# Norm squares summed in two rounded passes, low weight parts written over the loaded chunk, and another order of mixer steps, in a two-layer transformer kernel on one core

## What is computed

```python
def rms_norm(x, g):
    y = x * rsqrt(mean(x * x, axis=-1, keepdims=True) + 1e-6)
    return y * g

def mixer_block(h, ...):
    proj = rms_norm(h, norm1_g) @ w_in
    fq, fk, fv, ff, cq, ckv, krope, sq, sk, sv, gates = split(proj)
    fq, fk = rms_norm(fq per head of 64), rms_norm(fk per head of 64)
    log_decay = cumsum(log_sigmoid(ff + fox_forget_b))
    out_a = causal_attention(fq, fk, fv, log_decay)             # 8 heads (FOX)
    q = rope(rms_norm(rms_norm(cq) @ mla_w_q_up per head of 96))
    k, v_mla = from rms_norm(ckv) @ mla_w_kv_up and krope, k normed per head of 96, rope
    out_b = causal_attention(q, k, v_mla)                       # 8 heads (MLA)
    out_c = sliding_window_attention(rms_norm(sq), rms_norm(sk), sv, sinks, slopes)  # 8 heads (SWA)
    g = sigmoid(gates)
    return h + sum over branches(g * (out @ w_branch)) @ w_o

def conv_ffn(h, ...):
    u = rms_norm(h, norm2_g) @ w_up                             # 1024 to 5632
    c = conv_b + causal convolution of width 3 over tokens(u)
    gate, val = split(c)
    return h + (silu(gate) * val) @ w_down                      # 2816 to 1024
```

## Time and profile before

| what | before |
|---|---|
| median of three runs | 2064.24 us |
| the profiled execution, its own time | 2067.04 us |
| its span in the profile | 2065.2 us |
| PE busy | 1979.7 us (96%), 15080 matmuls |
| DVE / ACT / POOL busy | 1144.9 / 767.6 / 1023.8 us |
| mean granted PE clock | 0.988 of full speed |
| chain that ended last | PE 78%, DVE 11%, ACT 6%, issue 3% |

### The profile page before, as it was taken

One profiled execution on the slowest core, in us unless ns is written; L12 is line 12 of the kernel. 1 busy time (PEld: TensorE's weight loads), 2 busy tenths in 40 slices (PEclk: granted clock), 3 DMA queues, 4 the chain that ended last, 5 costly groups with the idle time before them and its releaser, 6 DMA issues.

```text
span 2065.2 us, 37779 instructions
## 1 busy us (share of the span) xinstructions
PE 1979.7 (96%) x15080; PEld 1879.0 (91%) x15080; DVE 1144.9 (55%) x2137; ACT 767.6 (37%) x1483; POOL 1023.8 (50%) x1306
## 2 busy tenths in 40 slices
PE   7899999899999999999998999999999999999999
PEld 7788997888999999999998889878889999999999
DVE  5665466676455665652356645656674656656411
ACT  4455566545222222220034555654452232222100
POOL 6755544443444444455476554543434445454543
PEclk9999999999999999999999999999999999999999
DMA  4112111111233323333332112111112323333332
GB/s 152 54 51 63 52 54 51 52 51 43 62 104 93 93 83 95 90 89 97 92 114 63 44 61 62 52 45 49 52 41 63 121 77 101 93 92 93 103 93 92
DMA packets 44803, 156.35 MB, mean 76 GB/s; under 512 B 5010, under 2 KB 5266, under 8 KB 44628
## 3 DMA queue, kind: packets, MB, share of 16 engines
q1 hardware_dynamic: 44484, 153.71, 24.6%
q10 hardware_dynamic: 144, 0.22, 0.0%
HBM read 149.58 MB, written 4.26 MB: 74 GB/s over the span
## 4 chain that ended last, share of the span: by engine, by line
PE 78%; DVE 11%; ACT 6%; issue 3%; DMA 0%; POOL 0%; ACTq 0%; DVEq 0%; SPq 0%
PE ps L1294 22%; PE ps L1297 21%; PE ps L1299 21%; PE ps L1528 5%; PE ps L1304 3%; DVE osum L1906 2%; DVE rstd L1619 1%; PE ps L1474 1%; PE ps L1435 1%; DVE ps L1876 1%; ACT xq L970 1%; DVE square L1614 1%; ACT square L987 1%; DVE q L1801 1%; ACT rstd L988 1%
## 5 line engine op out<-in xcount | busy, mean ns | idle before, releaser
L789 POOL TENSOR_TENSOR wl<-raw,wh 128x256 fp32r<-128x256 f32 x1080 | 800.6, 772 | 738.1 <-DVE wh L1598 729.9
L1294 PE MATMUL ps<-xh,wh 128*128 128x264 f32 (+1 forms) x2880 | 813.6, 304 | 5.8 <-POOL wl L789 2.7
L1297 PE MATMUL ps<-xl,wh 128*128 128x264 f32 (+1 forms) x2880 | 763.6, 285 | 0.0
L1299 PE MATMUL ps<-xh,wl 128*128 128x264 f32 (+1 forms) x2880 | 584.4, 284 | 0.0
L1294 PEld LDWEIGHTS ps<-xh,wh 128*128 128x128 f32 x2880 | 546.2, 190 | 32.7 <-issue 16.6
L1297 PEld LDWEIGHTS ps<-xl,wh 128*128 128x128 f32 x2880 | 546.5, 190 | 16.2 <-issue 7.2
L1299 PEld LDWEIGHTS ps<-xh,wl 128*128 128x128 f32 x2880 | 450.8, 190 | 0.0
L1598 DVE CAST wh<-raw 128x1024 fp32r<-128x1024 f32 x270 | 202.5, 750 | 166.1 <-PE ps L1294 152.2
L1898 DVE TENSOR_TENSOR ps<-ps,cst 128x128 f32<-128x128 f32 (+6 forms) x240 | 70.6, 296 | 209.7 <-PE ps L1480 139.6
L1297 PE MATMUL ps<-al,wh 128*128 128x264 f32 (+1 forms) x704 | 185.0, 283 | 0.0
L1294 PE MATMUL ps<-ah,wh 128*128 128x264 f32 (+1 forms) x704 | 183.6, 283 | 0.0
(11 more groups left out here) (183 smaller groups left out, 3208.1 us busy)
## 6 DMA issues: line engine op xcount, KB each, us to landing
raw<-weights SPq DMA_DIRECT2D x270, 512.0 KB, 3.6
h<-tokens SPq DMA_DIRECT2D x4, 528.0 KB, 6.5
h<-tokens SPq DMA_DIRECT2D x8, 264.0 KB, 5.3
residual<-h SPq DMA_DIRECT2D x8, 264.0 KB, 4.9
h<-residual SPq DMA_DIRECT2D x8, 264.0 KB, 5.9
out<-h SPq DMA_DIRECT2D x8, 256.0 KB, 4.7
cst<-constants SPq DMA_DIRECT2D x1, 1008.0 KB
extra<-positions SPq DMA_DIRECT2D x17, 4.1 KB
```

Source lines behind the costliest of these rows:

```text
L789: ins = nc.gpsimd.tensor_tensor(wl[c % SPLIT][:, part], raw[:, c % RAW, part], wh[c % SPLIT][:, part].bitcast(F32), ALU.subtract)
L1294: a = nc.tensor.matmul(out, a_hi, x_hi[:, sl], start=first, stop=False)
L1297: nc.tensor.matmul(out, a_hi, x_lo[:, sl], start=False, stop=False)
L1299: ins = nc.tensor.matmul(out, a_lo, x_hi[:, sl], start=False, stop=last)
```

## The change

**Squares in two parts.** ACT squares a normed tile twice from PSUM: first with a rounded output (`sqh`, fp32r), then in float32 (`sq`), and only then copies the tile to `rawt` (`mq` tiles have no copy). A new DVE step, "square low", subtracts one from the other in place and writes the rounded low part `sql` over `sq`. With `LAG` of -1 it stands on DVE directly behind the end of the tile, ahead of whatever else has that block position. The sum on PE waits for it (and for the copy, since it writes over the tile's PSUM) and is now two rounded passes, `sqh` and `sql`, against a rounded copy of the constants (`sums`), which ACT makes once at the start, over the float32 constants. The second pair of matmuls of an `mk` tile, the eight partial sums of the first residual norm and the sums of the residual norms stay float32.

**Low parts over the loaded chunk.** `raw` has four buffers instead of two, and POOL writes `wl` over `raw` in place; the three separate `wl` buffers are gone. A chunk of `raw` therefore stays in use until PE has multiplied by it: the load of chunk n now waits until PE has begun chunk n-3, which is one chunk later in SP's order than before (three chunks ahead of PE instead of four).

**Order.** `gF0` comes ahead of `fk0`, `fk1` ahead of `fq1`, `fq2` ahead of `fk2`, `gF2` ahead of `fq3`, `fv3` ahead of `gF3`, `gF6` ahead of `sq2`; `mv2` comes earlier and `mv3` later. Job 2 begins at block 127 instead of 121, jobs 1 and 11 one block later, jobs 7 and 8 two blocks earlier. The decay and rotation steps and a few lags move by some blocks.

```diff
@@ -32,7 +32,7 @@
-RAW, SPLIT = 2, 3
+RAW, SPLIT = 4, 3
...
-BEGIN = [65, 93, 121, 156, 192, 222, 250, 280, 318, 354, 391, 435]
+BEGIN = [65, 94, 127, 156, 192, 222, 250, 278, 316, 354, 391, 436]
...
-FIRST_LEAD, FIRST_STEP = 19, 1.0
-START = [16, 17, 16, 24, 30, 31, 2]
+FIRST_LEAD, FIRST_STEP = 16, 0.8
+START = [18, 18, 13, 21, 30, 32, 7]
...
             t.n = normed
             normed += 1
+            put(e + 1, 1, "square low", t)
...
+    raw_at = at[0]
     raw = sb("raw", [P, RAW, CW])
+    wl = sb("wl", [P, RAW, CW], F32R, offset=raw_at)
     wh = [sb(f"wh{i}", [P, CW], F32R) for i in range(SPLIT)]
-    wl = [sb(f"wl{i}", [P, CW], F32R) for i in range(SPLIT)]
...
+    sql = sb("sql", [P, 2, T], F32R, offset=sq_at)
+    sqh = sb("sqh", [P, 2, T], F32R)
...
+    sums = sb("sums", [P, 2 * P], F32R, offset=cst_at + CC_ONE * 4)
...
-                    sp.wait_ge(s_lo, n - RAW + 1)
+                    sp.wait_ge(s_start, n - RAW + 2)
...
-                    load(n // BLK + AHEAD + RAW)
+                    load(n // BLK + RAW - 1)
...
-                    ins = nc.gpsimd.tensor_tensor(wl[c % SPLIT][:, part], raw[:, c % RAW, part],
+                    ins = nc.gpsimd.tensor_tensor(wl[:, c % RAW, part], raw[:, c % RAW, part],
...
+            act.wait_ge(s_first, 16)
+            copy(sums[:, :], cst[:, CC_ONE:CC_ONE + 2 * P]).then_inc(sums_ready.sem, sums_ready.tick(()))
...
+                                nc.scalar.activation(sqh[0:MQ, t.n % 2, :], full(t.slot)[0:MQ, :], ACT.Square)
                                 nc.scalar.activation(sq[0:MQ, t.n % 2, :], full(t.slot)[0:MQ, :],
                                                      ACT.Square).then_inc(squared.sem, squared.tick((l, t.i)))
                             else:
+                                nc.scalar.activation(sqh[:, t.n % 2, :], full(t.slot), ACT.Square)
+                                nc.scalar.activation(sq[:, t.n % 2, :], full(t.slot),
+                                                     ACT.Square).then_inc(squared.sem, squared.tick((l, t.i)))
                                 for before in raw_before[t.i]:
                                     act.wait_ge(raw_taken.sem, raw_taken.at(l, before))
                                 copy(rawt[:, t.raw, :], full(t.slot)).then_inc(copied.sem, copied.tick((l, t.i)))
-                                nc.scalar.activation(sq[:, t.n % 2, :], full(t.slot),
-                                                     ACT.Square).then_inc(squared.sem, squared.tick((l, t.i)))
...
+            def stat_both(slot, i, lhs, rows, first=True, last=True):
+
+                stat(slot, sqh[0:rows, i, :], lhs[0:rows, :], first, False)
+                return stat(slot, sql[0:rows, i, :], lhs[0:rows, :], False, last)
...
-                        pe.wait_ge(squared.sem, squared.at(l, t.i))
-                        if t.kind == "mq":
+                        pe.wait_ge(square_low.sem, square_low.at(l, t.i))
+                        if t.kind != "mq":
+                            pe.wait_ge(copied.sem, copied.at(l, t.i))
+                        else:
                             pe.wait_ge(query_turned.sem, query_turned.at(l, t.i))
                         if t.kind == "cq":
-                            stat(t.slot, sq[:, (t.n - 1) % 2, :], ones, True, False)
-                            ins = stat(t.slot, sq[:, t.n % 2, :], ones, False, True)
+                            stat_both(t.slot, (t.n - 1) % 2, ones_r, P, True, False)
+                            ins = stat_both(t.slot, t.n % 2, ones_r, P, False, True)
                         elif t.kind == "mk":
                             if t.m == 0:
                                 pe.wait_ge(rope_squared.sem, rope_squared.at(l))
-                            stat(t.slot, sq[:, t.n % 2, :], pair, True, False)
+                            stat_both(t.slot, t.n % 2, pair_r, P, True, False)
                             ins = stat(t.slot, krr[ROPE:HD, :], ones[ROPE:HD, :], False, True)
                         elif t.kind == "mq":
-                            ins = stat(t.slot, sq[0:MQ, t.n % 2, :], ones[0:MQ, :])
+                            ins = stat_both(t.slot, t.n % 2, ones_r, MQ)
                         elif t.kind == "ckv":
-                            ins = stat(t.slot, sq[:, t.n % 2, :], ones)
+                            ins = stat_both(t.slot, t.n % 2, ones_r, P)
                         else:
-                            ins = stat(t.slot, sq[:, t.n % 2, :], pair)
+                            ins = stat_both(t.slot, t.n % 2, pair_r, P)
...
+                    elif s[0] == "square low":
+                        t = s[1]
+                        rows = MQ if t.kind == "mq" else P
+                        dve.wait_ge(squared.sem, squared.at(l, t.i))
+                        nc.vector.tensor_tensor(sql[0:rows, t.n % 2, :], sq[0:rows, t.n % 2, :],
+                                                sqh[0:rows, t.n % 2, :].bitcast(F32), ALU.subtract).then_inc(
+                            square_low.sem, square_low.tick((l, t.i)))
```

24 lines of the change are left out of this document (14 added, 10 removed).

## The result

The changed kernel takes 2104.42 us (median of four runs, 2103.61 to 2107.93), the kernel before 2066.02 in the same session; the ratio is 1.019, with a 95% interval of 1.0176 to 1.0204. It is slower by 38 us. The forecast was 2059.4 with a range of 2040 to 2080. The profiled execution has a span of 2106.1 us, 40.9 more than before.

A forecast was written before the change was run, and what follows sets the result against it. PE, busy 96% of the span, was taken as the bound. The terms -25.0 + 21.2 + 0 - 4.0 + 3.0 + 0 gave -4.8 us, from the median 2064.24 to 2059.4 us, range 2040 to 2080.

The forecast's parts named there:

- B: At the sums on PE: waits for the second square and the DVE subtraction cost +21.2 us, bounds 10.6 and 31.6.
- E: DVE standing at the subtraction delays casts, maxima and masks queued behind it: +3.0 us, bounds 0 and +18.
- A: Sums on PE: rounded matmuls in place of float32 save 12.5 us a layer, -25.0 us for both.
- C: Decays and PE's wait for the first value tile: 0 us, bounds -4 and +3.
- D: PE's wait at the shift of job 2 shrinks by 2.0 us a layer: -4.0 us, bounds 0 and -5.6.
- Rival 4: Sums on PE: two rounded passes take as long as one float32 pass; +20, 2084 us; chance 0.04.
- Rival 1: At the sums, steps between cover the waits, which fall to 5 us or less; -21, 2043 us; chance 0.15.
- Rival 2: DVE stands in order at the new step, delaying masks and maxima behind it; +10, 2074.4 us; chance 0.25.
- Rival 3: DVE and POOL exclude each other at SBUF, lengthening exposed subtractions; +8.6, 2068 us; chance 0.10.
- F: Later loads, in-place low parts and the constants' copy: 0 us, bounds -1 and +4.

The follow-up runs named there:

- e5: Kernel before with the new loads and the new tables, float32 sums kept: 2081.85 us (ratio 1.0081).
- e3: Changed kernel without the DVE subtraction; the second pass sums the rounded squares again: 2072.89 us (ratio 1.0037).
- e17: Changed kernel with the subtraction cut to 8 of 528 columns and the low part left out of the sum: 2086.25 us.
- e13: e10 with DVE's four rotation steps two positions later, behind fk1's subtraction: 2107.86 us.
- e15: Kernel before with float32 sums, new tables and new loads, the load of chunk 7 ahead of the decays' DMAs: 2083.27 us (ratio 1.0085).
- e9: Kernel before with the new loads, the decays' DMAs two positions later on SP's queue, behind the load of chunk 7: 2065.32 us (ratio 0.9997).
- e4: Kernel before with the new loads alone (four raw buffers, low part in place, load issued three chunks ahead): 2080.16 us (ratio 1.0079).
- e1: Changed kernel with the old tables (order, job begins, starts, lags, leads): 2114.85 us (ratio 1.0241).
- e14: Kernel before's tables with all sums in two parts and new loads, the load of chunk 7 ahead of the decays' DMAs: 2107.41 us (ratio 1.0203).
- e10: Changed kernel with START[2] at 18, so the load of chunk 7 stands ahead of the decays' DMAs: 2105.87 us.
- e18: Changed kernel with another DVE operation of the same size ahead of the subtraction, so the step is twice as long: 2149.61 us (ratio 1.041).
- e16: Kernel before with squares rounded by ACT and summed in one rounded pass, low part left out, no DVE step: 2053.74 us (ratio 0.994).
- e11: e9 with two-part sums only for six tiles (fk3, sq0, cq0, cq1, ckv0, mk1): 2072.45 us (ratio 1.0019).

## Why the prediction was wrong, step by step

Three steps failed. The new DVE step (B and E) with the shorter sums (A) was put at -0.8 us and measures +22 behind the new order, +42 behind the old. The waits that it makes lie at the sums and the shifts, where the subtraction waits for DVE's queue, and not at the masks, where E had them. The order (C and D) was put at -4 and costs 18 by itself on float32 sums, with waits for exponentials that had no term. And the clock at half speed, through which both cost much of what they cost, had no term in the sum (the range had two stretches, 7 us) and took 24.7. How the waits of PE behind the start move along the way (us in total by what is waited for, summed from the list of waits of each):

| | before | e5, order and loads | e3, two passes | e17, step of 0.17 us | changed kernel |
|---|---|---|---|---|---|
| at the sums | 19.3 | 12.1 | 18.6 | 29.4 | 40.9 |
| for the shifts | 7.0 | 6.9 | 6.2 | 10.9 | 10.4 |
| for the value tiles | 8.7 | 6.5 | 6.6 | 8.2 | 9.2 |
| for maxima | 10.4 | 12.9 | 11.4 | 6.5 | 8.4 |
| for exponentials | 11.7 | 21.4 | 23.8 | 25.3 | 21.9 |

**A, the shorter sums: right in kind, short in size.** -25.0 was forecast, the work at full clock fell by 19.9. A sum without a wait, in the changed kernel:

```profile
139.72 0.41 PE L1320 MATMUL ps<-sqh,sums 128*128 128x264 f32 x2
139.97 0.40 PE L1320 MATMUL ps<-sql,sums 128*128 128x264 f32 x2
140.20 0.17 PE L1497 MATMUL ps<-xq,xk 97*16 97x16 f32 x1
```

It takes 140.20 - 139.72 = 0.48 us, as worked out from the earlier trace rows. A sum that has waited takes 0.59 to the next instruction, and 30 of 54 wait for the low part: some 3.3 of the 5.1 us that are missing. The rest stays open. Rival 4, which had no gain at all, is out.

**B, the sums' waits: the size right partly by luck.** +21.2 was forecast, 19.3 to 40.9 is +21.6. But the order alone had taken 7 us off these waits (e5), so two squares and the step brought 29, and some tiles paid nothing where others paid several times their price. At the late MLA query tiles the working holds; the timeline at mq4:

```profile
453.55 0.60 ACT L1038 ACTIVATE sq<-ps 96x528 f32<-96x528 f32 x1
...
454.94 0.71 DVE L1771 TENSOR_TENSOR rawt<-ps,gq 32x528 f32<-32x528 f32 x1
...
455.69 0.70 DVE L1811 TENSOR_TENSOR sql<-sq,sqh 96x528 fp32r<-96x528 f32 x1
...
456.45 0.51 PE L1320 MATMUL ps<-sqh,sums 96*128 96x264 f32 x2 [1.85 <-DVE sql L1811]
```

Second square, two products, subtraction, and PE 0.06 us behind it: it waited 1.85 us where before it waited 0.67, 1.18 more against the 1.22 forecast. (The subtraction stands behind the products, not ahead of them; for PE that is the same.) At mq5 to mq7 the waits are 1.0, 0.9 and 1.4 us longer. But fk1, which I priced at half of 0.75, pays 3 us:

```profile
62.32 0.72 DVE L1621 CAST wh<-raw 128x1024 fp32r<-128x1024 f32 x1 [2.21 <-DMA raw<-weights]
...
66.54 0.60 ACT L1042 ACTIVATE sq<-ps 128x528 f32<-128x528 f32 x1
...
69.81 1.14 DVE L1871 TENSOR_TENSOR krr<-gsb,krr 32x528 f32<-32x528 f32 x1
...
70.98 1.02 DVE L1811 TENSOR_TENSOR sql<-sq,sqh 128x528 fp32r<-128x528 f32 x1
...
72.05 0.81 PE L1320 MATMUL ps<-sqh,sums 128*128 128x264 f32 x2 [4.35 <-DVE sql L1811]
```

Here DVE waits for chunk 7, does rotation steps back to back, comes to the subtraction only at 70.98, and PE has waited 4.35 us. ACT's second square had ended at 67.14. Until now this sum hung on ACT, which is busy for 37% of the span, and waited 1.37 us. I priced what would queue behind the new step and the step's own length, and left out what stands ahead of it: the sum now waits for DVE's whole queue. e13 shows that by moving what stands ahead. e17 shows it too: with hardly any length, the step makes this sum wait 2.97 us, where e3, without the step, waits 0.08.

```profile
71.73 0.95 PE L1320 MATMUL ps<-sqh,sums 128*128 128x264 f32 x4 [2.97 <-DVE sql L1811]
```

Rival 1, the steps between cover it, is out by the same waits.

**C, the first value tile:** 0 forecast, +0.5 for both layers, of which the order alone is -2.2 (e5) and two squares and the step +2.7. **D, the shift of job 2: wrong in sign.** -4.0 was forecast, the waits at the shifts rose by 3.4. The timeline at job 2 (`vt`, then `nmm`, then PE's shift):

```profile
125.77 0.70 DVE L1748 SCALAR_TENSOR_TENSOR vt<-ps,hsum 128x528 f32<-128x528 f32 x1
...
126.39 0.16 DVE L1884 CUSTOM_DVE_ANT_0 ps<-ps,cst 16x16 f32<-16x16 f32 x1
...
126.80 0.28 PE L1466 MATMUL ps<-cst,nmm 16*128 16x16 f32 x1 [4.57 <-DVE nmm L1884]
```

I took the six blocks more of distance for time won. In DVE's order the norm's steps moved along, the copy `vt` now stands directly ahead of `nmm`, and a subtraction joined the queue; the wait is 4.57 us where the earlier trace rows had 2.81. The order alone gives no gain here: in e5 this wait is 3.15 us. The rise comes with the step: 2.38 in e3, 4.77 in e17. What the order costs lies elsewhere. e5 has

```profile
PE ps L1444 <- DVE nmm L1855: 6.9, 4, 3.2
...
PE ps L1475 <- ACT ptm L1194: 5.8, 2, 3.0
```

for the shifts and for exponentials (`ptm`); before, the latter were four waits of 1.0 us at most, 3.4 in all. With the order alone (e15) PE idles 4.9 us more than in e9, and 20 more are lost to half clock, between profiled executions that lie 23 us apart where the medians lie 18. Four of its 15 half-clock stretches, the two longest (10.2 us) among them, begin during or just behind waits of 2.6 to 3.0 us for exponentials. Which table entry does that was not tried.

**E, DVE standing at the step: too small.** The rows of the step (ns min/median/max, and DVE's idle time before it) and one of its stands:

```profile
L1811 DVE TENSOR_TENSOR sql<-sq,sqh x56: 680/708/1298, 34.1 to 1575.9; 128x528 fp32r<-128x528 f32 x40, 96x528 fp32r<-96x528 f32 x16
...
  ACT sq L1042: 64.5, 29
```

```profile
113.84 0.61 ACT L1042 ACTIVATE sq<-ps 128x528 f32<-128x528 f32 x1
...
114.48 0.71 DVE L1811 TENSOR_TENSOR sql<-sq,sqh 128x528 fp32r<-128x528 f32 x1 [1.98 <-ACT sq L1042]
```

ACT's second square ends at 114.45, DVE had stood for 1.98 us, and at 29 subtractions it stood for 64.5 us in all. In e17 the standing and the link alone cost 13.4 us by the medians; the waits at its sums are 29.4 us, of which 4.4 are for the copy, 11.3 in all beyond those of e3 (18.1 in its two rows). E looked for the price at masks and exponentials; there the step adds nothing clear (23.8 us in e3, 25.3 in e17, 21.9 in the changed kernel), and the waits are at the sums and the shifts. Rival 2 had the sign and the standing, but put the price at masks and maxima (the waits for maxima fell, too), and gave +10 over the old time where the whole is +38. **Rival 3**, the shared access: the Trainium skill, page "SBUF — State Buffer", section "SBUF: two separate sides", has a DVE operation with two SBUF inputs and a GpSimd operation that reads SBUF shut each other out for a whole instruction. The trace agrees: 14 of the 56 subtractions take more than 0.8 us, up to 1.298, and each of these began while a GpSimd instruction ran. But the median is 0.708 us, and all that goes beyond it is 5.0 us over 56 subtractions, not all of it at sums for which PE waits, where rival 3 had 8.6. By its own sign (a median well over 0.7) it is out. In e17, 13 of 56 are held up as well, by 5.5 us, so up to that much of its 13.4 may be this and not the standing.

**F, the loads: wrong on the kernel before, without effect in the changed one.** The text had it ("the decays' DMAs stand one load earlier in SP's queue") and costed it at 0, because PE still had two chunks made. The reader of that chunk that mattered was DVE, whose order is shared with all that PE waits for. It is worth 14 to 15 us on the kernel before (e4 and e9), 7.4 with two-part sums under the old order (e1 and e14), and nothing on the changed kernel (e10).

**The clock: the term that was missing.** The range allowed for two half-clock stretches, 7 us. There are 18 in place of 8, and they cost 24.7 us more. 17 of the 18 begin during a wait of PE of 1.4 us or longer or within 2.5 us behind its end; at fk1 the clock fell during the wait of 4.35 us. That is no rule for single waits: before, with 14 such waits behind the start, only 4 of the 8 stretches begin there. The Trainium skill, page "TensorE: Matmul & The Clock Gate", section "Part 1: The HAM clock gate (the "warmup" mystery)", has the same two levels and an idle engine falling to the lower. The trace agrees on the levels, and in the changed kernel on the fall in or just behind a wait. By how much the lost time can exceed the idle time is shown by e4 against e9: 5.1 us less idle time went with 13.7 us less lost to the clock.

**The sum by medians.** Order and loads (e5) +17; two rounded passes with two squares and a later copy (e3) -9; a step on DVE to stand at (e17) +13; its length (changed kernel) +18: 39 in all. The forecast had C, D and F, which stand for order and loads, at -4 in place of +17. For all that hangs on the squares it had A, B and E, -25.0 + 21.2 + 3.0 = -0.8; they measure -9 + 13 + 18 = +22. This is one way through the change. The other way gives other shares: loads without their fault 0 (e9), two-part sums under the old order +42 (e14), the new order -1.5 (e10). In both the squares are the larger part, and they were put at -0.8.

**The range.** Its high end doesn't follow from its terms: -25.0 + 31.6 + 0 + 6 + 7 for two stretches is +20, which gives 2084, not 2086. It also took E at 6 of its 18 and left out the upper bounds of C and F.

## What to carry to other kernels

When a wait is moved to another engine, price that engine's whole queue, what stands ahead of the new step as well as what stands behind it; the step's own length cost six tenths of itself at first, and more than itself when it was doubled, once the spare time was gone (e17, e18). A transfer that the bounding engine needs late may be needed early by another engine that walks its steps in order. And on a bound TensorE count idle time and clock together: waits of some microseconds can cost again at half clock (here 24.7 us lost to it beside 36.2 more idle), so work taken off TensorE where it soon waits for others is worth a fraction of its length (here a third, e16). Two changes that each cost time alone need not cost their sum: here the order alone cost 18 us, two-part sums alone 42, and both together 40, since an order is good or bad for the waits that are there (e15, e14, e10).

## What the runs showed of the hardware

A float32 sum of 128 rows by 264 columns in two halves kept PE for 0.91 us (less the product between), two rounded passes for 0.48, one rounded pass for 0.25. All 14 subtractions of DVE that were held up (more than 0.8 us instead of 0.708) had begun while a GpSimd instruction ran. Half-clock time did not follow idle time evenly: 5.1 us of idle time less went with 13.7 us less lost to the clock (e9 against e4), while the profiled execution of e11, with less idle time than that of e9 (86.0 against 86.9), lost 9.3 us more to it. Nor is it fixed for a kernel: the runs of e11 have mean granted clocks from 0.979 to 0.991, and its time moves with them by 19 us. Neither could be predicted from these traces.
